# Folding the last layer's conditioning columns on VectorE ahead of one matmul with ones

## The chip, the cores and the metric

The kernel runs on 1 core of a Trainium2 chip, in one launch. The metric is the device time of one execution in microseconds; the kernel before was timed in three runs.

## The reference

A backbone of two layers over 256 latent tokens and 256 context tokens of 1024 channels, all in float32. Each layer takes a conditioning vector `c`, turns it into six vectors of 1024 (shift, scale and gate for each of two sub-layers), and uses them around a token mixer and a mixture of experts:

```
silu_c = silu(c)
for layer in range(2):
    mx = split(silu_c @ ada_w[layer] + ada_b[layer], 6)      # ada_w[layer] is 1024 x 6144
    hx = rms_norm(x, g0) * (1 + mx[1]) + mx[0]
    z = hx @ w_in[layer]                                     # 1024 x 1952: queries, keys, values of four head groups
    o = mix(z) @ w_out[layer]
    x = x + mx[2] * rms_norm(o, g1)
    h = rms_norm(x, g2) * (1 + mx[4]) + mx[3]
    x = x + mx[5] * rms_norm(moe(h), g3)                     # 16 experts, 2 of one group per token
```

The context tokens go the same way with a conditioning vector of their own, but in the last layer they only give keys and values. So of the last layer's six vectors the context stream uses only the first two.

## The kernel before

Each layer runs as a chain of stages: input projection (`project`), second projections of the latent head group (`latent_projections`), attention (`mix`), output projection (`project_out`), routing, experts, and `combine`, which adds the experts' rows and prepares the next layer's tokens. Layer 1 is the last one.

The conditioning is a product of a 2 x 1024 matrix with a 1024 x 6144 one. The weight matrix `ada_w[L]` is cut into 12 items of 2 MB, `("ada", L, i)`. Three rounds `r` of four items give 2048 columns each: r=0 shift and scale of the mixer, r=1 gate of the mixer and shift of the experts, r=2 scale and gate of the experts. In one item the channel index of partition p is 8p + k, with two values of k. `ada_item` (L464) does one item on TensorE: for both k and four column groups g, a matmul with the 32 columns of `silu_c` as the stationary operand and 512 weight columns as the moving one, accumulated in one PSUM bank (B_ADA). Each float32 matmul shows as two instructions in the trace, so an item has 16. After four items VectorE copies the bank to SBUF (`ada_rows`, L1290), TensorE turns it in four transposes (`ada_turn`, L483), and VectorE adds the bias and makes the gains (`ada_columns`, L1298 to L1311).

For layer 1, round 0 is done in layer 0's attention. Items 4 to 11 are done between the layers and in layer 1's input projection: item 4 ahead of `turn_combined(L, 0)`, items 5 and 6 after the tiles cq0 and cq1, item 7 at the end of the first weight chunk, item 8 after the second, items 9 and 10 after the third, item 11 after the fourth.

The order between the layers is this. `combine` has two halves: the latent tokens (s=0) and the context tokens (s=1). For each, VectorE adds the experts' rows and normalises (L1642 to L1669), with row statistics from ScalarE (L1204 to L1208, L965 to L969). TensorE then turns the rows (`turn_combined`, L884), and ScalarE applies scale and shift on the way out of PSUM (`modulate_combined`, L994). Input projections of layer 1 follow in four weight chunks: cq0, cq1, ckv, kr | bk, bv, bq0, bq1 | dq0, dk0, dq1, dk1 | dv0, dv1, u0, u1. Of cq, bq, dq and u only the 256 latent tokens are computed, of the others all 512. The engines run their programs in order and wait on semaphores for named events: "staged" (a weight item has landed), "used" (its buffer may be overwritten), "filled" and "read" (a PSUM bank).

SyncE issues all weight loads in one queue, in the order of `items`. The six staging buffers are thirds of `W[0]` (0 to 2) and `W[1]` (3 to 5), 16 KB a partition each. A load waits for "used" of the item that had the buffer last. `R1` is a region of 4096 columns that holds the experts' rows in `combine`, and later, in attention, the probabilities. Layer 1's queries, keys and values are written into `W[0]`, that is over the staging buffers 0 to 2.

On VectorE, layer 1 starts with `ada_rows(1, 1)` and `ada_columns(1, 1)`, then `latents` (the gains of cq and ckv, L1336 and L1339), then `ada_rows(1, 2)`, then the rotary embeddings (`rope`, L1321 to L1330, with the copies at L1346).

Of the kernel before, what the change touches and what calls it, by code (L numbers as in the profile page):

```python
# [24 lines left out]
D = 1024  # L25
# [137 lines left out]
def hybrid_block(nc, A, out, known=None):  # L163
    ctx = ExitStack()
    with ctx:
# [70 lines left out]


        h_scaled = [part(R1, i * D, D) for i in range(2)]
        amp2_row, gate1_row = part(R1, 2 * D, D), part(R1, 3 * D, D)
# [138 lines left out]
        for L in range(DEPTH):  # L378
# [4 lines left out]
            for i in range(HEADS):  # L383
# [9 lines left out]
        stage1 = [(("in", 1, 0), 3), (("in", 1, 1), 4), (("in", 1, 2), 5), (("ada", 1, 4), 1), (("ada", 1, 5), 2),  # L393
                  (("ada", 1, 6), 1), (("ada", 1, 7), 0), (("in", 1, 3), 3), (("ada", 1, 8), 0), (("ada", 1, 9), 4),
                  (("ada", 1, 10), 0), (("ada", 1, 11), 5), (("out", 1, 0), 3), (("out", 1, 1), 4)]
        items += [it for it, _ in stage1]
# [40 lines left out]
        def _(pe):  # L437
# [25 lines left out]
            def ada_item(S, it):  # L463
# [12 lines left out]
                mm.then_inc(*mark(S, ("used", item_no[it])))  # L476

            def ada_turn(S, L, r):

                pe.wait_ge(*at("ada_sb", L, r))  # L480
                t = take("adaT", L, r)
                for q in range(4):
                    mm = nc.tensor.transpose(t[:, q * P:(q + 1) * P], ada_sb[:, q * P:(q + 1) * P], ident)  # L483
                mm.then_inc(*mark(S, ("filled", "adaT", L, r)))

            def project(L):
# [25 lines left out]
                for c, names in enumerate((("cq0", "cq1", "ckv", "kr"), ("bk", "bv", "bq0", "bq1"),  # L512
# [4 lines left out]
                    if c == 0 and L:  # L517

                        for name in ("cq0", "cq1"):
                            tile(name, w, take(name, L), 0, SEQ).then_inc(*mark(S, ("filled", name, L)))  # L520
                        for i in (5, 6):
                            ada_item(S + "_ada", ("ada", 1, i))
                        turn_combined("pe_comb1", L, 1)
                        t = {name: take(name, L) for name in ("ckv", "kr")}
                        for lo in (0, SEQ):
                            for name in ("ckv", "kr"):
                                mm = tile(name, w, t[name], lo, lo + SEQ)
                                if lo:
                                    used = [("used", item_no[it])] if name == "kr" else []
                                    mm.then_inc(*mark(S, ("filled", name, L), *used))  # L530
                        ada_item(S + "_ada", ("ada", 1, 7))
                        continue
                    for name in names:
# [13 lines left out]
                        if used and L == 0 and c:  # L547
                            ada_item(S + "_ada", ("ada", 0, 3 + c))
                        if used and L:
                            for i in {1: (8,), 2: (9, 10), 3: (11,)}[c]:  # L550
                                ada_item(S + "_ada", ("ada", 1, i))
                            if c == 1:
                                ada_turn(S + "_turn", 1, 1)
                        if name == "bk":
# [354 lines left out]
            for L in range(DEPTH):  # L909
                if L:  # L910
                    ada_item("pe_comb", ("ada", 1, 4))
                    pe.wait_ge(*at("banks_out", L - 1))
                    turn_combined("pe_comb", L, 0)
# [26 lines left out]
        def _(act):  # L940
# [61 lines left out]
            def project(L):  # L1002
# [10 lines left out]
                for g in range(4):  # L1013
                    keys = [("read", "kr", L), ("tile", L, "kr")] if g == 3 else []
                    a(kr[64:96, g * P:(g + 1) * P], src[MLA_ROPE * g:MLA_ROPE * (g + 1), 0:P], ACT.Copy).then_inc(*mark(S, *keys))
                copy(S, bks[L], ("bk", L), keys=[("tile", L, "bk")])
                finish_rstd(S, ("cq", L), 1, (0, nq), 256, ("ckvn", L - 1) if L else None)
                square(S, ("ckv", L), 0, ckv, NTOK, 0)
                copy(S, bvs[L][:, :, :].rearrange("p t c -> p (t c)"), ("bv", L), keys=[("v", L, "swa")])
                for j in range(2):  # L1020
                    src = read(act, f"bq{j}", L)
                    for b in range(2 if nq > SEQ else 0):
                        a(bqz[L][64 * b:64 * b + 64, 2 * b + j, SEQ:nq], src[64 * b:64 * b + 64, SEQ:nq], ACT.Copy, scale=SWA_SCALE)
                    a(bqs[L][:, j, :], src[:, 0:SEQ], ACT.Copy, scale=SWA_SCALE)\
                        .then_inc(*mark(S, ("read", f"bq{j}", L), ("tile", L, f"bq{j}")))
                finish_rstd(S, ("ckv", L), 0, (0, NTOK), 128, ("cqn", L))
                for j in range(2):
                    copy(S, dqs[L][:, j, 0, 0:nq], (f"dq{j}", L), nq, scale=DIFF_SCALE, keys=[("tile", L, f"dq{j}")])
# [14 lines left out]
            def latent_projections(L):  # L1043
                S, nq = f"act_lat{L}", q_tokens(L)
                for h in range(HEADS):
                    copy(S, qas[L][0:MLA_QK, h, 0:nq], ("qa", L, h), nq, hi=MLA_QK, scale=MLA_SCALE, keys=[("tile", L, f"qa{h}")])
# [234 lines left out]
        def _(v):  # L1281
# [3 lines left out]
            def ada_rows(S, L, r):  # L1285

                v.wait_ge(*at("used", item_no[("ada", L, 4 * r + 3)]))
                if (L, r) != (0, 0):
                    v.wait_ge(*at("filled", "adaT", *((L, r - 1) if r else (L - 1, 2))))
                nc.vector.tensor_copy(ada_sb[:, :], psum[:, B_ADA, :]).then_inc(*mark(S, ("ada_sb", L, r)))  # L1290

            def ada_columns(S, L, r):
# [39 lines left out]
            def latents(L):  # L1332
# [6 lines left out]
                stt(ckv, ckv, vecT[:, 68 + L:69 + L], rstd[:, :], ALU.mult, ALU.mult).then_inc(*mark(S, ("ckvn", L)))  # L1339
                if L:  # L1340
                    ada_rows(S, 1, 2)
                rope(S, L, "kr")
# [377 lines left out]
            for L in range(DEPTH):  # L1720
                if L:
                    ada_rows("v_seam", 1, 1)
                    ada_columns("v_seam", 1, 1)
                latents(L)
# [10 lines left out]
        def _(g_):  # L1735
            gt = nc.gpsimd.tensor_tensor

            def zero_queries(L):

                g_.wait_ge(*at("filled", "ckv", L))  # L1740
                nc.gpsimd.memset(bqz[L][64:P, 0:2, :], 0.0)
                nc.gpsimd.memset(bqz[L][0:64, 2:4, :], 0.0).then_inc(*mark(f"g_rope{L}", ("q_zero", L)))
# [161 lines left out]
        def _(sp):  # L1904
# [26 lines left out]
            for L in range(DEPTH):  # L1931
# [16 lines left out]
                for n in range(lo, hi):  # L1948
                    if items[n] == ("ada", 1, 7):
                        for tt in range(4):  # L1950
# [62 lines left out]
```

## Time and profile before

| What | Value |
|---|---|
| Runs | 1197.90, 1199.62, 1202.74 us (median 1199.62) |
| Profiled execution | 1200.96 us, of which the trace's span is 1199.1 |
| TensorE matmul busy | 950.8 us, 79% |
| VectorE busy | 316.3 us, 26% |
| ScalarE busy | 266.5 us, 22% |
| GpSimd busy | 171.0 us, 14% |
| DMA, mean over the span | 269 GB/s |
| Mean granted TensorE clock | 0.903 |

A granted clock of 1.00 is 2.4 GHz, one of 0.50 is 1.2 GHz. "Busy" says how long an engine had an instruction under way; what bounds a stage is read from which wait ends last in it. The change lies between 680 and 800 us of the span; the experts of layer 0 lie before it, attention and the experts of layer 1 behind it.

### The profile page before, as it was taken

How to read it: one execution, taken by the hardware profiler on the slowest of the kernel's cores; microseconds unless marked ns; L12 is line 12 of the kernel's file. 1: busy time of each engine (PE TensorE's matmuls, PEld its weight loads, DVE VectorE, ACT ScalarE, POOL GpSimd, SP SyncE). 2: the span in 40 equal slices, each digit the busy share in tenths (PEclk: the TensorE clock that was granted, in tenths of full speed). 3: DMA queues.
4: the chain of work that ended last, by engine and by line, in shares of the span. 5: the costliest groups of instructions: out<-in, count | busy, mean ns of one | idle time of the engine just before them, and what ended most of it. 6: DMA issues, size and time to landing. Idle time of an engine off the chain costs nothing. (4 is left out here: it accounts for less than half of the span.)

```text
span 1199.1 us, 23394 instructions
## 1 busy us (share of the span) xinstructions
PE 950.8 (79%) x8976; PEld 601.0 (50%) x8977; DVE 316.3 (26%) x893; ACT 266.5 (22%) x712; POOL 171.0 (14%) x256
## 2 busy tenths in 40 slices
PE   4899998999997699989974289998996585655561
PEld 2454646766554466656752166657754353422240
DVE  1100064457434211111110420046635110000003
ACT  4121033546332111101100241024632100000001
POOL 0010025000021222211210220013001211100011
PEclk9999997999997799999997599998997788877796
DMA  9982333570175799999999945230129999999983
GB/s 376 333 254 101 140 141 141 211 247 1 34 283 208 274 372 410 410 411 410 411 411 404 357 160 234 107 140 1 38 89 371 374 410 409 410 410 410 409 326 136
DMA packets 97333, 323.04 MB, mean 269 GB/s; under 512 B 11946, under 2 KB 22964, under 8 KB 90996
## 3 DMA queue, kind: packets, MB, share of 16 engines
q1 hardware_dynamic: 70528, 279.19, 59.0%
q0 software_dynamic: 9600, 31.81, 7.8%
q10 hardware_dynamic: 17140, 11.13, 3.0%
q8 instruction: 46, 0.75, 0.2%
q14 instruction: 19, 0.16, 0.0%
HBM read 309.58 MB, written 18.81 MB: 274 GB/s over the span
## 5 line engine op out<-in xcount | busy, mean ns | idle before, releaser
L825 PE MATMUL psum<-weights,lat 128*32 128x256 f32 x2688 | 181.3, 426 | 96.7 <-DMA weights<-in_exp_w_gu_dram 59.5
L825 PEld LDWEIGHTS psum<-weights,lat 128*32 128x32 f32 x2688 | 108.8, 121 | 163.9 <-issue 131.5
L508 PE MATMUL psum<-hT,weights 128*128 128x512 f32 (+1 forms) x336 | 120.7, 518 | 5.6 <-ACT lat L1000 3.2
L1607 DVE STREAM_TRANSPOSE lat<-lat 128x256 f32<-128x256 f32 x66 | 29.4, 446 | 355.1 <-PE psum L825 342.6
L1169 ACT ACTIVATE lat<-psum 128x128 f32<-128x128 f32 x64 | 17.7, 277 | 357.6 <-PE psum L825 355.4
L508 PEld LDWEIGHTS psum<-hT,weights 128*128 128x128 f32 x336 | 64.0, 192 | 59.3 <-issue 49.1
L838 PE MATMUL psum<-weights,lat 128*32 128x256 f32 x1344 | 83.7, 387 | 4.7 <-issue 4.0
L659 PE MATMUL psum<-weights,R 128*128 128x64 f32 x480 | 68.8, 286 | 11.3 <-ACT R L1084 7.1
L1851 POOL DMA_INDIRECT lat<-h_rows,slot_col x68 | 66.5, 978 | 53.9 <-POOL slot_col L1848 53.0
L1380 DVE TENSOR_REDUCE st<-psum 128x1 f32<-128x512 f32 (+1 forms) x96 | 56.7, 599 | 61.9 <-PE psum L628 28.3
L659 PEld LDWEIGHTS psum<-weights,R 128*128 128x128 f32 x480 | 64.2, 205 | 16.1 <-ACT R L1084 10.9
L474 PE MATMUL psum<-weights,silu_c 128*32 128x512 f32 x384 | 49.2, 634 | 29.1 <-DMA weights<-in_ada_w_dram 29.1
L838 PEld LDWEIGHTS psum<-weights,lat 128*32 128x32 f32 x1344 | 53.5, 112 | 26.8 <-issue 6.5
L1071 ACT ACTIVATE R<-psum,st 128x512 f32<-128x512 f32 (+1 forms) x78 | 48.0, 616 | 84.8 <-DVE st L1380 53.3
L737 PE MATMUL psum<-weights,hT 128*128 128x512 f32 x144 | 65.3, 608 | 0.2 <-ACT hT L1108 0.2
L1848 POOL COPY slot_col<-slots 128x1 int32 (+1 forms) x68 | 12.4, 183 | 366.3 <-DVE lat L1607 348.8
L825 PE MATMUL psum<-hT,lat 128*32 128x256 f32 x672 | 46.3, 418 | 22.8 <-DMA hT<-in_exp_w_gu_dram 10.7
L825 PE MATMUL psum<-R,lat 128*32 128x256 f32 x672 | 43.7, 399 | 8.9 <-DMA R<-in_exp_w_gu_dram 8.9
L1175 ACT ACTIVATE lat<-psum 128x256 f32<-128x256 f32 x63 | 24.1, 383 | 102.6 <-PE psum L838 101.0
L825 PEld LDWEIGHTS psum<-hT,lat 128*32 128x32 f32 x672 | 26.6, 118 | 39.0 <-issue 31.4
L1000 ACT ACTIVATE weights<-psum 128x512 f32<-128x512 f32 (+4 forms) x36 | 20.1, 559 | 112.9 <-PE psum L508 51.0
L737 PEld LDWEIGHTS psum<-weights,hT 128*128 128x128 f32 x144 | 27.5, 195 | 32.4 <-issue 32.1
(260 smaller groups left out, 1161.0 us busy)
## 6 DMA issues: line engine op xcount, KB each, us to landing
weights<-in_exp_w_gu_dram SPq DMA_DIRECT2D x44, 2048.0 KB, 23.9
weights<-in_ada_w_dram SPq DMA_DIRECT2D x24, 2048.0 KB, 8.7
weights<-in_exp_w_down_dram SPq DMA_DIRECT2D x22, 2048.0 KB
hT<-in_exp_w_gu_dram SPq DMA_DIRECT2D x10, 2048.0 KB
R<-in_exp_w_gu_dram SPq DMA_DIRECT2D x10, 2048.0 KB, 25.7
spare_w<-in_exp_w_down_dram SPq DMA_DIRECT2D x10, 2048.0 KB, 24.3
weights<-in_w_in_dram SPq DMA_DIRECT2D x6, 2048.0 KB, 16.5
weights<-in_w_out_dram SPq DMA_DIRECT2D x4, 2048.0 KB, 9.1
```

Of the source, the lines that this page charges most:

```text
L474: mm = nc.tensor.matmul(psum[32 * g:32 * g + 32, B_ADA, :], silu_c[:, k, :], w[:, k2, g, :], start=(k == 0), stop=(k == 7), skip_group_che ...
L508: mm = nc.tensor.matmul(t[:, lo:hi], w[:, k, col:col + P], hT[:, k, lo:hi], start=(k == 0), stop=(k == KD - 1))
L659: mm = nc.tensor.matmul(t[:, 0:64], probT[u % 2][:, i, :], v, start=(i == 0), stop=(i == n - 1))
L737: nc.tensor.matmul(t, mixT[:, k, tt * P:(tt + 1) * P], w[:, k, :], start=(k == 0), stop=False)
L825: mm = nc.tensor.matmul(gu_ps[BLK * j:BLK * j + BLK, 0:256], xgT[:, k, :], w[:, k % 4, j, :, :, :], start=(k == 0), stop=(k == KD - 1), sk ...
L838: mm = nc.tensor.matmul(y_ps[BLK * j:BLK * j + BLK, 0:256], actT[:, b, :], w_dn[place][:, b, j * 256:(j + 1) * 256], start=(b == 0), stop= ...
L1000: a(dst, src, ACT.Copy, scale=scale).then_inc(*mark(S, ("read", *job), *keys))
L1071: a((prob[u % (AHEAD + 1)] if v == 0 else prob2)[:, 0:nk], read(act, "s", L, u, v)[:, 0:nk], ACT.Exp, bias=s_[:, v:v + 1], accum_out=s_[:, ...
L1175: a(y_sb[par], psum[:, 3, 0:256], ACT.Copy).then_inc(y_copied, 1)
L1380: ins = red(s_[:, j:j + 1], read(v, "s", L, u, j)[:, 0:nk], AX.X, ALU.max, negate=True)
L1607: nc.vector.transpose(xgT[:, :, :].rearrange("p k s -> p (k s)"), xg[par]).then_inc(x_ready, 1)
L1851: g_.indirect_dma_start(xg[par], None, h_parts, bass.IndirectOffsetOnAxis(ap=slot_col[:, par:par + 1], axis=0))\
```

## The change

For items 4 to 11 of layer 1, TensorE's matmuls are taken out. VectorE instead multiplies each weight block of 128 partitions x 2048 columns by the one column of `silu_c` that belongs to it and adds it to an accumulator of 128 x 2048 in `R1` (`ada_fold`: one tensor_scalar and seven scalar_tensor_tensor a round). Then four matmuls with 32 columns of ones sum the accumulator over the partitions into bank B_ADA (`ada_sum`). Only the latent stream's vectors come out, which is all that the last layer uses of these rounds. The copy, the turn and the columns stay, at other places. The staging buffers of items 6, 7, 11 and of the second output weights change, "used" of an ada item is now told by VectorE, and ScalarE and GpSimd get waits where they write over a staging buffer.

```diff
+        ada_acc = part(R1, 0, 2 * D)
...
-        stage1 = [(("in", 1, 0), 3), (("in", 1, 1), 4), (("in", 1, 2), 5), (("ada", 1, 4), 1), (("ada", 1, 5), 2),
-                  (("ada", 1, 6), 1), (("ada", 1, 7), 0), (("in", 1, 3), 3), (("ada", 1, 8), 0), (("ada", 1, 9), 4),
-                  (("ada", 1, 10), 0), (("ada", 1, 11), 5), (("out", 1, 0), 3), (("out", 1, 1), 4)]
+        stage1 = [(("in", 1, 0), 3), (("in", 1, 1), 4), (("in", 1, 2), 5), (("ada", 1, 4), 1), (("ada", 1, 5), 2),
+                  (("ada", 1, 6), 0), (("ada", 1, 7), 2), (("in", 1, 3), 3), (("ada", 1, 8), 0), (("ada", 1, 9), 4),
+                  (("ada", 1, 10), 0), (("ada", 1, 11), 4), (("out", 1, 0), 3), (("out", 1, 1), 5)]
...
+            def ada_sum(S, L, r):
+                pe.wait_ge(*at("folded", L, r))
+                reuse(B_ADA, ("ada_sb", L, r))
+                for g in range(4):
+                    mm = nc.tensor.matmul(psum[32 * g:32 * g + 32, B_ADA, :], ones[:, 0:32], ada_acc[:, g * 512:(g + 1) * 512],
+                                          start=True, stop=True, skip_group_check=True)
+                mm.then_inc(*mark(S, ("ada_sum", L, r)))
...
-                        for i in (5, 6):
-                            ada_item(S + "_ada", ("ada", 1, i))
...
-                        ada_item(S + "_ada", ("ada", 1, 7))
...
-                        if used and L:
-                            for i in {1: (8,), 2: (9, 10), 3: (11,)}[c]:
-                                ada_item(S + "_ada", ("ada", 1, i))
-                            if c == 1:
-                                ada_turn(S + "_turn", 1, 1)
+                        if L and name == "bq0":
+                            ada_sum(S + "_ada", 1, 1)
+                        if L and name == "dk1":
+                            ada_turn(S + "_turn", 1, 1)
+                        if L and name == "dv0":
+                            ada_sum(S + "_ada", 1, 2)
...
-                    ada_item("pe_comb", ("ada", 1, 4))
...
+                if L:
+                    act.wait_ge(*at("used", item_no[("ada", 1, 4)]))
                 copy(S, bks[L], ("bk", L), keys=[("tile", L, "bk")])
...
+                if L:
+                    act.wait_ge(*at("used", item_no[("ada", 1, 7)]))
                 for j in range(2):
                     copy(S, dqs[L][:, j, 0, 0:nq], (f"dq{j}", L), nq, scale=DIFF_SCALE, keys=[("tile", L, f"dq{j}")])
...
+                if L:
+                    act.wait_ge(*at("used", item_no[("ada", 1, 10)]))
                 for h in range(HEADS):
                     copy(S, qas[L][0:MLA_QK, h, 0:nq], ("qa", L, h), nq, hi=MLA_QK, scale=MLA_SCALE, keys=[("tile", L, f"qa{h}")])
...
+            def ada_fold(S, L, r):
+                for k in range(KD):
+                    it = ("ada", L, 4 * r + k // 2)
+                    w, c = staged(it)[:, k % 2, :, :].rearrange("p g n -> p (g n)"), silu_c[:, k, 0:1]
+                    used = [("used", item_no[it])] if k % 2 else []
+                    if k % 2 == 0:
+                        v.wait_ge(*at("staged", item_no[it]))
+                    if k == 0:
+                        ts(ada_acc, w, c, None, ALU.mult).then_inc(*mark(S, ("fold", L, r, k)))
+                    else:
+                        v.wait_ge(*at("fold", L, r, k - 1))
+                        stt(ada_acc, w, c, ada_acc, ALU.mult, ALU.add)\
+                            .then_inc(*mark(S, ("fold", L, r, k), *used, *([("folded", L, r)] if k == KD - 1 else [])))
...
                 if L:
+                    ada_rows(S, 1, 1)
+                    ada_fold(S, 1, 2)
+                    ada_columns(S, 1, 1)
                     ada_rows(S, 1, 2)
                 rope(S, L, "kr")
...
                 if L:
-                    ada_rows("v_seam", 1, 1)
-                    ada_columns("v_seam", 1, 1)
+                    v.wait_ge(*at("filled", "yT", 1, 0, KD // 2 - 1))
+                    ada_fold("v_seam", 1, 1)
                 latents(L)
...
                 g_.wait_ge(*at("filled", "ckv", L))
+                if L:
+                    g_.wait_ge(*at("used", item_no[("ada", 1, 4)]))
...
-                    if items[n] == ("ada", 1, 7):
+                    if items[n] == ("ada", 1, 6):
                         for tt in range(4):
                             sp.wait_ge(*at("x", 0, 2, tt))
                     load(n)
```

## Rows read from the trace of the kernel before

**Rows 1.** Page, busy time, share of the span and instructions of each engine.

```profile
PE 950.8 (79%) x8976; PEld 601.0 (50%) x8977; DVE 316.3 (26%) x893; ACT 266.5 (22%) x712; POOL 171.0 (14%) x256
```

**Rows 2.** Chain of waits, 600 to 960 us: start, us, what, instructions.

```profile
705.66 3.69 PE psum L508 x16
...
716.75 1.72 PE psum L474 x14
718.46 7.06 PE psum L508 x16
...
740.59 1.85 PE psum L474 x16
...
743.89 20.64 PE psum L508 x64
764.53 3.57 PE psum L474 x32
768.10 14.01 PE psum L541 x64
...
789.02 1.90 PE psum L474 x16
790.94 0.55 DVE spare_w L1290
```

**Rows 3.** Timeline, seam between the layers: start us, us, engine, line, idle before.

```profile
680.22 0.75 DVE L1669 TENSOR_SCALAR R<-x_tok,rs 128x1024 f32<-128x1024 f32 x1 [1.12 <-ACT rs L969]
...
682.94 3.64 PE L474 MATMUL psum<-weights,silu_c 128*32 128x512 f32 x16 [28.35 <-DMA weights<-in_ada_w_dram]
...
686.51 2.15 PE L884 MATMUL psum<-cst,R 128*128 128x128 f32 x16
...
687.46 3.75 ACT L994 ACTIVATE hT<-psum,mod,amp 128x256 f32<-128x256 f32 x8 [7.26 <-PE psum L884]
...
688.50 7.07 PE L508 MATMUL psum<-hT,weights 128*128 128x256 f32 x32
...
691.06 1.09 ACT L1204 ACTIVATE spare_w<-spare_w 128x1024 f32<-128x1024 f32 x1
...
695.50 3.64 PE L474 MATMUL psum<-weights,silu_c 128*32 128x512 f32 x32
...
699.68 0.75 DVE L1669 TENSOR_SCALAR spare_w<-x_tok,rs 128x1024 f32<-128x1024 f32 x1 [1.11 <-ACT rs L969]
```

**Rows 4.** TensorE by stretches: length, busy, instructions, granted clock, DMA share, GB/s.

```profile
625.00:626.00 1.00, 0.00 (x0) 0.75 1.06 414
823.00:824.00 1.00, 0.47 (x2) 0.74 0.00 0
682.90:686.50 3.60, 3.56 (x16) 0.50 0.94 396
699.20:705.60 6.40, 1.94 (x16) 1.00 0.94 370
1000.00:1050.00 50.00, 29.13 (x468) 0.86 1.03 410
```

**Rows 5.** VectorE groups by form: busy us, mean ns; idle before.

```profile
L1645 DVE SCALAR_TENSOR_TENSOR R<-R,rs 128x1024 f32<-128x1024 f32 x4 | 5.1, 1284 | 3.0 <-DMA R<-y_rows,spos 3.0
...
L1339 DVE SCALAR_TENSOR_TENSOR lat<-lat,vecT,spare_w 128x512 f32<-128x512 f32 x2 | 1.5, 752 | 24.0 <-ACT spare_w L959 24.0
```

**Rows 6.** Timeline, 803 to 806 us: VectorE additions without and with GpSimd beside them.

```profile
804.50 0.42 DVE L1330 TENSOR_TENSOR weights<-R 96x256 f32<-96x256 f32 x1
...
805.09 0.63 POOL L1755 TENSOR_TENSOR R<-weights,cst 96x256 f32<-96x256 f32 x1 [5.90 <-DVE weights L1330]
805.29 0.72 DVE L1330 TENSOR_TENSOR weights<-R 96x256 f32<-96x256 f32 x1
```

**Rows 7.** Staged loads: all of L1912, and those of the conditioning, 620 to 1000 us.

```profile
DMA to landing us min/median/max: 7.2/10.3/33.0
...
weights<-in_ada_w_dram SPq DMA_DIRECT2D x8, 2048.0 KB, 9.5
```

More of the change, by code:

```diff
@@ L1285, in ada_rows @@
             def ada_rows(S, L, r):
-                v.wait_ge(*at("used", item_no[("ada", L, 4 * r + 3)]))
+                if L and r:
+                    v.wait_ge(*at("ada_sum", L, r))
+                else:
+                    v.wait_ge(*at("used", item_no[("ada", L, 4 * r + 3)]))
                 if (L, r) != (0, 0):
@@ L1290, in ada_rows @@
                 nc.vector.tensor_copy(ada_sb[:, :], psum[:, B_ADA, :]).then_inc(*mark(S, ("ada_sb", L, r)))
+            def ada_fold(S, L, r):
[7 more added lines that the diff above has]
+                        ts(ada_acc, w, c, None, ALU.mult).then_inc(*mark(S, ("fold", L, r, k)))
+                    else:
+                        v.wait_ge(*at("fold", L, r, k - 1))
+                        stt(ada_acc, w, c, ada_acc, ALU.mult, ALU.add)\
+                            .then_inc(*mark(S, ("fold", L, r, k), *used, *([("folded", L, r)] if k == KD - 1 else [])))
             def ada_columns(S, L, r):
```

## The prediction

> **What bounds the kernel now.** The page comes first: TensorE is busy for 79% of the span [rows 1], a mean over stages that differ. The chain of waits from 600 to 960 us shows the stage that is touched: from 705.66 to 790.94 it is TensorE alone, input-projection matmuls with the conditioning's (L474) between them, with no wait for another engine [rows 2]. What goes from TensorE there, goes from the path. The timeline of the seam shows the stretch before it [rows 3]. TensorE's first work of the layer is item 4, which waits for its load until 682.94, while the rows for the first turn are ready after VectorE's 680.22 + 0.75 = 680.97. The turn (L884) starts at 686.51. ScalarE modulates behind it until 691.21, and only then takes the statistics of the context rows (691.06), because its program runs in order; these lead to the last scaled rows at 700.43, and to the projection at 705.66. Attention follows from 790.94. Layer 1's experts move weights at 410 GB/s with the DMA engines full (share 1.03) [rows 4]; their first loads wait for the end of attention, so the whole DMA-bound stretch moves with it and gives nothing back.
>
> **Item 4 leaves the seam.** The turn can start at about 681.05 in place of 686.51: 5.46 us earlier. But item 4's 3.64 us ran at a granted clock of 0.50 [rows 3, 4], that is 1.2 GHz, and the turn behind it at 2.4 GHz. Now the turn itself meets the low clock. Its 2.15 us become about 4.3; ScalarE follows one bank behind, so its 3.75 us of modulation end some 0.7 us later against the turn's start. 5.46 - 0.7 = 4.76 us are left for the chain through ScalarE and VectorE to 705.66.
>
> **Items 5 and 6** (695.50, 3.64 us) lie where TensorE would otherwise wait for the scaled rows until 700.43 [rows 3]. Removed, they give nothing.
>
> But TensorE is now busy less. Its projection of cq ends near 693 to 694; then it waits to about 695.7, turns for 1.94 us, and waits some 3.2 us more for ScalarE. In the trace the clock fell at 625 and at 823, in or just after idle gaps of 2 to 3 us, but held through 699.20 to 705.60, which had 1.94 us of work in 6.40 [rows 4]. The new stretch is 1 to 2 us longer with the same work in it. I take it that the clock falls once. Where it fell, it came back after 3 to 7 us; 3.2 us of projection at half rate lose 1.6 us, and the chance that the second turn is caught as well adds 0.2. The bounds are 0 and 3.5 (a fall of 7 us). I take 1.8, since the projection that follows is dense. 4.76 - 1.8 = **2.96 us**.
>
> **Items 7 to 11 leave the projection.** They are on the path at 1.71 (716.75 to 718.46), 1.86, 3.57 and 1.90 us [rows 2]: 9.04. The two sums bring back four matmuls of 512 columns each, half an item, so half of 1.85: 0.9 each, 1.8 together. The turn of round 1 (0.6 us) only moves. 9.04 - 1.8 = **7.2 us**.
>
> **VectorE's copy leaves the path.** Before, rope waited behind the copy of 0.55 us that followed item 11 at 790.94 [rows 2]. Now the second sum is done two tiles earlier, and VectorE waits for the rotation of kr itself. That gives about **0.45 us**; bounds 0 and 0.6.
>
> **The folds and their cover.** Two forms bound the price: scalar_tensor_tensor takes 1284 ns for 1024 columns and 752 for 512 [rows 5], so 1.04 ns a column plus 0.22, and 2.35 us for 2048. The first step, with one tensor operand, takes 0.75 us for 1024 [rows 3], so between 1.3 and 1.5. A fold is 1.4 + 7 x 2.38 = 18 us. VectorE is idle for most of the stage, so this costs nothing if each fold is ready when its sum is due.
>
> The first starts at about 697.5 - 1.8 = 695.7, behind the scaled rows. Item 6 now waits for the last x rows (near 693) and lands by 702. Item 7 waits on SyncE for the buffer of item 5, that is for the fourth step (704.4); queued behind it are the last input chunk, which waits for its own buffer until about 712 anyway, and item 8. Item 7 lands 7.2 to 9.5 us after its issue [rows 7], near 712 to 714, so the fold ends at 717 to 719. Its sum is due after bq0: 11.1 us of first chunk, then 22.1 - 1.9 - 3.5 us, near 732. Cover: 12 us. Queued behind it on VectorE are the gains of cq, which need statistics that are not ready before about 720.
>
> The second starts after ckv's gain and the copy of round 1, near 740.6, and ends at 758.4 if nothing lacks. Its items form a chain. Item 9 waits for the second chunk's buffer (736.8) and lands at 744.0 to 746.3, where step 3 is due at 744.3. Item 10 waits for step 2 (744.3) and lands at 751.5 to 753.8. Item 11 takes item 9's buffer, so it waits for step 4 (749 to 751) and lands at 756 to 760.5. The fold ends at 761 to 765.5. Its sum is due after dv0: the third chunk's 20.64, 0.6 of turn and 7.0 of dv0 [rows 2] after 737.7, near 765.9. Cover: 0.4 to 4.9 us. So it costs nothing, narrowly.
>
> The added waits of ScalarE and GpSimd are for items 4 and 7 (done by 700 and 719, asked at about 720 and 739) and item 10 (done near 757, asked near 780): nothing. The larger accumulator is written over rows of R1 that are used up, and gone before attention's probabilities.
>
> **A rule against the change.** A VectorE addition of 256 columns takes 0.42 us alone and 0.72 with a GpSimd operation beside it [rows 6]. The Trainium skill's "GPSIMD Engine Reference", section 1, says that GpSimd shares its SBUF interfaces with VectorE, with contention for VectorE instructions that have two SBUF inputs; seven of the eight steps are such. By that rule the folds could stretch wherever GpSimd works; this trace agrees for short additions.
> By rows 6 alone a step beside GpSimd work would take 0.72 / 0.42 = 1.7 times as long. In the first fold GpSimd has about 2.3 us of work (two fills and two cosines), which adds 1 to 2 us inside a cover of 12. In the second it has none, because its next cosine waits for kr's rope.
>
> **Sum.** 2.96 + 7.2 + 0.45 = 10.6 us. The profiled execution took 1200.96, so its like would take 1190.4; the three runs' median is 1.34 lower, which puts the median at 1189.0.
>
> **Rivals.**
> - The clock does not fall in the seam: 12.4 us gained, 1187.2. For it speaks 699.20 to 705.60, against it the two other gaps [rows 4].
> - The second fold is late: loads land slower than 9.5 us, which the maximum of 33.0 shows possible [rows 7], though the DMA engines are nearly free here; or steps take 1.7 times as long [rows 6], which makes the fold 31 us and its end near 772. TensorE then waits 3 to 7 us at the second sum, and everything behind waits too: 1192 to 1196, say 1194.5.
> - The seam gives nothing: another wait takes item 4's place in front of the turn. I see none (bank release is long past), but then 7.6 us remain: 1192.
> - Slower: the steps on 2048 columns run far slower than the slope of two shorter forms says. The second fold ends at 740.6 + 8 steps; the gain is eaten when it ends 10.6 us after 765.9, that is at 4.5 us a step, and 6 us more are lost at 5.2. Price at 6 us a step: 740.6 + 48 = 788.6, 22.7 late, 12 us slower: 1212. Nothing in [rows 5] points to it.
>
> **How the numbers follow.** Forecast 0.49; no fall 0.29; late fold 0.12; seam without gain 0.06; slower 0.04. A measurement of this kernel tells about 0.5% from no change, so faster means under 1193.6: the first two, the fourth, and part of the third, less some doubt for the sizes: 0.85. Within 0.5%: 0.11. Slower: 0.04. The range takes in the second case with 2.5 us of spread below and the late fold's middle above: 1184.5 to 1195.
>
> **What would show it.** In the changed trace: the first L884 near 681 at a clock of 0.50; the projection of ckv starting near 702.7 (700.9 without a fall); steps of 2.35 us; TensorE without a gap at both sums; rotation of kr near 780; then attention's end and the first expert load some 10.6 us earlier. The prediction is wrong if TensorE is idle before the second sum, if steps are longer, or if the clock stays low past 706.

## The result and the profile after

The changed kernel took 1183.36 us (median of four runs, 1181.96 to 1188.72); the kernel before beside it took 1198.76 (four runs, 1195.94 to 1202.74). The ratio is 0.9875, with a 95% interval of 0.9839 to 0.9911. Nine further runs of the changed kernel, against 25 of the kernel before, gave a ratio of 0.9917 (0.9884 to 0.9951). The forecast was 1189.0 in a range from 1184.5 to 1195: the direction was right, and the median of the first four runs fell 1.1 us below the range. Where the missing time came from is the question of this document.

The page of the changed kernel, busy time by engine, answers to [rows 1]: TensorE has 15.8 us less, VectorE 35 us more.

```profile
PE 935.0 (79%) x8864; PEld 596.0 (50%) x8865; DVE 351.3 (30%) x909; ACT 267.1 (23%) x712; POOL 172.1 (15%) x256
```

Its chain of waits from 720 us on answers to [rows 2] (start, us, what, instructions; L518, L548 and L510 are the projection's matmuls, L484 is `ada_sum`, L493 the turn, L573 the rotation).

```profile
725.15 0.99 PE psum L484 x8
726.15 3.60 PE psum L510 x32
729.75 1.05 PE psum L461 x2
730.81 20.64 PE psum L518 x64
751.45 0.44 PE psum L493 x4
751.88 6.91 PE psum L548 x32
758.79 1.00 PE psum L484 x8
759.79 7.10 PE psum L548 x32
766.89 6.91 PE psum L518 x32
773.80 0.56 PE psum L573 x2
```

No item is left on TensorE, each sum takes 1.0 us, and TensorE goes from tile to sum to tile without a wait. The rotation of kr starts at 773.8 where it was 790.8. The timeline of the seam answers to [rows 3]:

```profile
672.81 0.76 DVE L1703 TENSOR_SCALAR R<-x_tok,rs 128x1024 f32<-128x1024 f32 x1 [1.12 <-ACT rs L976]
...
673.83 3.31 PE L892 MATMUL psum<-cst,R 128*128 128x128 f32 x16 [28.67 <-DVE R L1703]
...
675.02 3.76 ACT L1001 ACTIVATE hT<-psum,mod,amp 128x256 f32<-128x256 f32 x8 [2.24 <-PE psum L892]
...
687.93 1.59 DVE L1317 TENSOR_SCALAR R<-weights,silu_c 128x2048 f32<-128x2048 f32 x1
688.11 3.65 PE L892 MATMUL psum<-cst,spare_w 128*128 128x128 f32 x16 [4.07 <-DVE spare_w L1703]
...
689.55 12.03 DVE L1320 SCALAR_TENSOR_TENSOR R<-weights,silu_c,R 128x2048 f32<-128x2048 f32 x5
...
693.71 5.38 PE L518 MATMUL psum<-hT,weights 128*128 128x256 f32 x16 [1.95 <-ACT lat L1007]
```

The first turn now starts 0.26 us after its rows (673.57) and not 5.54 us after. The first ckv tiles take 5.38 us where they took 3.69. TensorE by stretches shows why, as in [rows 4] (length, busy times of the engines, granted clock, DMA share, GB/s):

```profile
676.00:686.00 10.00, 8.04 (x39) 6.86 (x38) 6.96 (x7) 7.99 (x20) 0.23 (x1) 0.97 0.12 51
686.00:697.00 11.00, 6.94 (x24) 5.97 (x25) 9.60 (x7) 6.08 (x16) 6.13 (x8) 0.54 0.78 265
698.00:706.00 8.00, 8.00 (x82) 6.70 (x82) 5.50 (x3) 0.60 (x1) 1.04 (x2) 1.00 0.62 251
```

Behind the first turn the clock fell once, for some 10 us, and came back in the ckv tiles.

To see where the time went, both spans are cut at the same events of the timelines: SyncE's first expert load of layer 0, the scaled rows of the latent stream, the first turn (L884, L892), the last scaled rows, the first ckv tile, the rotation of kr, and the first expert load of layer 1.

| Stretch, us | before | after | difference |
|---|---|---|---|
| start to first expert load of layer 0 | 325.48 | 318.11 | -7.37 |
| to the scaled rows of the latent stream | 355.49 | 355.46 | -0.03 |
| to the first turn | 5.54 | 0.26 | -5.28 |
| to the last scaled rows | 13.92 | 14.18 | +0.26 |
| to the first ckv tile | 5.23 | 5.70 | +0.47 |
| to the rotation of kr | 85.15 | 80.02 | -5.13 |
| to the first expert load of layer 1 | 99.80 | 99.67 | -0.13 |
| to the end | 308.49 | 307.80 | -0.69 |
| span | 1199.1 | 1181.2 | -17.9 |

The five stretches from the scaled rows to layer 1's first expert load hold the change, and in this pair of profiles they are 9.8 us shorter. The largest difference, 7.37 us, lies in the first quarter of the kernel, where the two programs do the same work.

### The profile page after: what moved, and what is told of

It is laid out like the page before. It is cut to its first block and busy times, and to the rows that moved or that the text cites. A ratio compares the mean times of both kernels' runs of the same rounds, so it can differ in the third digit from the quotient of the medians.

```text
span 1181.2 us, 23197 instructions
## 1 busy us (share of the span) xinstructions
PE 935.0 (79%) x8864; PEld 596.0 (50%) x8865; DVE 351.3 (30%) x909; ACT 267.1 (23%) x712; POOL 172.1 (15%) x256
## 5 line engine op out<-in xcount | busy, mean ns | idle before, releaser
L518 PE MATMUL psum<-hT,weights 128*128 128x512 f32 (+1 forms) x336 | 122.4, 524 | 3.5 <-ACT lat L1007 1.9
L518 PEld LDWEIGHTS psum<-hT,weights 128*128 128x128 f32 x336 | 65.2, 196 | 57.2 <-issue 48.3
L667 PE MATMUL psum<-weights,R 128*128 128x64 f32 x480 | 65.6, 277 | 11.4 <-ACT R L1097 7.1
L667 PEld LDWEIGHTS psum<-weights,R 128*128 128x128 f32 x480 | 60.9, 196 | 16.2 <-ACT R L1097 10.9
L833 PE MATMUL psum<-hT,lat 128*32 128x256 f32 x672 | 46.3, 416 | 22.5 <-DMA hT<-in_exp_w_gu_dram 10.6
L1655 DVE STREAM_TRANSPOSE lat<-lat 128x128 f32<-128x128 f32 x64 | 20.0, 312 | 81.6 <-PE psum L846 80.2
```

What stands on the lines that cost most here:

```text
L518: mm = nc.tensor.matmul(t[:, lo:hi], w[:, k, col:col + P], hT[:, k, lo:hi], start=(k == 0), stop=(k == KD - 1))
L667: mm = nc.tensor.matmul(t[:, 0:64], probT[u % 2][:, i, :], v, start=(i == 0), stop=(i == n - 1))
L833: mm = nc.tensor.matmul(gu_ps[BLK * j:BLK * j + BLK, 0:256], xgT[:, k, :], w[:, k % 4, j, :, :, :], start=(k == 0), stop=(k == KD - 1), sk ...
```

## The experiments

### Is the first quarter part of the change?

Theory A: the change is worth what its own stretches show, about 10 us, and the rest is where the TensorE clock falls in layer 0, which differs from run to run. Theory B: the change moves layer 0 too and is worth 15 us. Both kernels were run again, unchanged.

> The kernel before, unchanged, timed against itself. Theory A (the change is worth about 10.5 us, and what the medians show beyond that is where the TensorE clock happens to fall in layer 0, which both kernels share): runs spread over some 1194 to 1203 us, and the first expert load of layer 0 (325.5 us before, 318.1 us in the changed kernel's trace) lies anywhere between 317 and 326. Theory B (the change also moves layer 0 for good): that load stays within 1 us of 325.5 and the runs within 1197 to 1202.

> The changed kernel, unchanged, timed against the kernel before. Theory A: ratio 0.990 to 0.992 (9.5 to 12 us less), with layer 0's first expert load anywhere between 317 and 326 us of the trace. Theory B: ratio 0.987 or less (15 us), with that load again near 318.

The kernel before, against itself: ratio 1.0 (0.9973 to 1.0026). Its twelve runs form two groups: four from 1191.0 to 1192.9 and eight from 1198.3 to 1200.3. Not every set is parted so sharply: beside the fills below, the same kernel also had runs at 1194.4, 1194.6 and 1195.6. The changed kernel: 0.9917 (0.9884 to 0.9951), which at 1198 us is 9.9 us; two runs at 1181.1 and 1181.3 and seven from 1188.3 to 1192.1. Group against group the change is worth 9 to 11 us. In its second profile the changed kernel had its first expert load of layer 0 at 324.40 us, not at 318.11: it does not keep the early one. The kernel before was again late, at 324.29. The range expected for before (1194 to 1203) was too narrow below.

TensorE by stretches, in the first profile of the changed kernel (length, busy, granted clock, DMA share, GB/s):

```profile
184.00:188.00 4.00, 0.23 (x2) 1.00 0.49 209
188.00:192.00 4.00, 4.00 (x15) 0.57 0.01 4
192.00:202.00 10.00, 10.00 (x82) 1.00 0.42 149
```

And in its second profile, the same kernel:

```profile
184.00:188.00 4.00, 0.47 (x3) 0.96 0.43 180
188.00:202.00 14.00, 14.00 (x56) 0.52 0.01 1
202.00:204.00 2.00, 2.00 (x18) 1.00 0.75 176
```

TensorE waits 3.9 us for VectorE in both, and the clock falls within 1 us of the end of that wait in both. In one it comes back within 4 us, in the other it stays at 1.2 GHz for 14 us though TensorE is busy throughout. Of the first ten profiles five had the long one, with the load at 322.9 to 325.5. In the other five, with the load at 316.5 to 318.1, the clock was low for 3 to 4 us in four and for 7 us in one (the seam alone, below). Both kinds are spread over kernels with and without the change.

The long stretch is most of the 7.37 us, but not all. When TensorE comes out of that wait, the kernel before is 0.87 us behind. Over the next attention matmuls, up to the end of the long stretch, it loses 4.9 us more. The last 1.6 us come later, where its clock fell twice before the expert load (0.76 in 285 to 290 us, 0.81 in 305 to 310) and that of the changed kernel once (0.66 in 300 to 305).

### Filling the gap in layer 0

```diff
+                    if L == 0 and i == 6:
+                        for _ in range(4):
+                            nc.tensor.matmul(psum[0:30, B_ADA, :], silu_c[:, 0, 2:32], C("inv_count"), start=False, stop=False, skip_group_check=True)
                     if i > AHEAD:
                         values(i - AHEAD - 1)
```

The columns 2 to 31 of `silu_c` are zero, so this adds zeros. It was put into both kernels.

> The kernel before with TensorE fed in one gap of layer 0: its wait of 3.9 us for VectorE at about 185 us of the trace gets four matmuls of 512 columns with a stationary block of zeros, added to the conditioning bank. In five of the ten profiles so far the clock that falls at that gap stays low for 14 us, in the others for 3 to 4, with the first expert load at 323 to 325.5 or at 316.5 to 318. Theory A (this draw is what splits the runs of every kernel here into two groups 7 us apart): with the gap filled the clock holds at 1.00 there, the first expert load comes at 318 or earlier, the runs form one group, near 1191 to 1193 where the kernel before has most of them at 1198 to 1200. If the groups come from elsewhere, two groups remain.

> The changed kernel with the same fill in layer 0. Theory A: one group near 1181 to 1182, and against the kernel before with the same fill 10 us less, which is the change's worth without the draw of layer 0 (10.6 predicted). Theory B (the change is worth 15): 15 us less than the kernel before with the fill.

The kernel before with the fill, TensorE by stretches:

```profile
184.00:188.00 4.00, 3.63 (x16) 1.00 0.09 31
188.00:192.00 4.00, 3.42 (x27) 1.00 0.00 0
192.00:202.00 10.00, 10.00 (x84) 1.00 0.58 211
```

The clock holds, there and up to the first expert load, which comes at 313.8 us (313.9 in the changed kernel). Before with the fill: 1191.96 us (twelve runs, ten of them 1188.9 to 1193.9, two at 1196.3 and 1199.0). Its ratio to the unfilled kernel beside it is 0.9969 (0.9945 to 0.9993), a gain of 3.7 us. Changed kernel with the fill: 1180.49 (six runs, 1179.5 to 1185.2), ratio 0.9877 (0.9844 to 0.991) to the unfilled kernel before. Between the two filled kernels the difference of the medians is 11.5 us, of the means 11.0, with a standard error of 1.3 from the spread of the runs (an estimate). So with this draw filled, the change is worth what its own stretches say, and 15 us is unlikely. The fill moves most runs of the kernel before into the lower group, so layer 0's clock accounts for most of the split. It does not remove it: a spread of some 5 us and two runs above it stay, and in the last experiment below the filled kernel still had its load at 317.2, with two later falls of the clock.

The profiles show a second such place, which I had not looked for. In attention of layer 1, too, TensorE has one wait of 2.2 us for ScalarE. In the first profile of the changed kernel (one row of the timeline, one of TensorE by stretches):

```profile
806.27 1.92 PE L667 MATMUL psum<-weights,R 128*128 128x64 f32 x8 [2.22 <-ACT R L1097]
806.20:813.00 6.80, 6.73 (x27) 0.51 0.00 0
```

And at the same place in the kernel of the next experiment:

```profile
814.44 1.10 PE L660 MATMUL psum<-weights,R 128*128 128x64 f32 x8 [2.21 <-ACT R L1084]
814.40:821.20 6.80, 6.76 (x49) 1.00 0.00 0
```

After the same wait the clock fell in one and held in the other. From the rotation of kr to the first expert load of layer 1 the thirteen profiles took 99.5 to 99.9 us (seven), 98.0 (two) or 96.4 to 96.7 (four). This is a draw of up to 3 us inside the stretches that I had counted as the change's own. Both kernels, three profiles each (unchanged, unchanged again, with the fill):

| us | scaled rows to rotation | rotation to expert load | together |
|---|---|---|---|
| before | 109.84, 110.37, 110.05 | 99.80, 99.67, 99.70 | 209.64, 210.04, 209.75 |
| after | 100.16, 99.70, 100.89 | 99.67, 98.02, 97.98 | 199.83, 197.72, 198.87 |

Up to the rotation the means differ by 9.8 us. Together they differ by 11.0, and 1.2 of that is how the clock fell in layer 1's attention. Whether the change makes a fall there less likely, three profiles each do not tell.

### The seam alone

The kernel before, with all items on TensorE, the changed kernel's staging buffers and SyncE's wait at item 6, and this order:

```diff
-                    ada_item("pe_comb", ("ada", 1, 4))
...
-                        for i in (5, 6):
+                        for i in (4, 5):
                             ada_item(S + "_ada", ("ada", 1, i))
...
-                        ada_item(S + "_ada", ("ada", 1, 7))
+                        for i in (6, 7):
+                            ada_item(S + "_ada", ("ada", 1, i))
```

> The kernel before with only the seam changed: all items stay matmuls on TensorE, with the changed kernel's staging buffers; items 4 and 5 come after the cq tiles, 6 and 7 after the first chunk. The first turn starts 0.3 us after its rows where it took 5.5 to 6.3, and items 4 and 5 keep TensorE busy where it would idle. Expected: 5.3 us gained in front of the turn, 0.3 lost behind it (low clock in the turn), item 6 on the path for 1.8: 3.2 us faster than before, 87.0 us from the ckv tiles to the rotation of kr, ckv tiles at full clock (3.7 us for 16). If the fold itself is needed for the seam's gain, no gain.

Ratio 0.9958 (0.9917 to 0.9999). The first turn starts 0.26 us after its rows, so the gain in front of the turn does not need the fold; it needs item 4 out of the way. The last scaled rows follow in 14.17 us. But from the ckv tiles to the rotation it took 89.7 us, not 87.0, and TensorE's timeline shows why:

```profile
683.25 3.64 PE L474 MATMUL psum<-weights,silu_c 128*32 128x512 f32 x32
686.82 1.97 PE L885 MATMUL psum<-cst,spare_w 128*128 128x128 f32 x16
691.98 6.55 PE L508 MATMUL psum<-hT,weights 128*128 128x256 f32 x16 [3.19 <-ACT lat L1000]
```

The ckv tiles ran at the low clock (6.55 us in place of 3.69), in spite of items 4 and 5 in front. The clock fell in the 3.19 us before them, a gap that it had survived in [rows 4]. My expectation that the items would hold it was wrong. There was a second loss. The cq tiles in front took 8.10 us, the clock being low in part of them, so items 4 and 5 ended late and the second turn started 0.87 us after its rows (685.95). From the scaled rows to the rotation this kernel took 110.18 us, against 109.84 in the kernel before: all of the 5.28 us were lost again behind the turn. That the whole was faster still is in line with the two draws: its profile had one of the shorter falls in layer 0 and none in layer 1's attention (96.58 us). So moving the items alone does not keep the gain of the seam; why the clock did not survive the gap here is open.

### Half of the fold

Round 1 folded, round 2 back on TensorE: `ada_fold(S, 1, 2)` and its sum are gone, and

```diff
+                        if L and name == "dk0":
+                            ada_item(S + "_ada", ("ada", 1, 8))
+                        if used and L and c > 1:
+                            for i in {2: (9, 10), 3: (11,)}[c]:
+                                ada_item(S + "_ada", ("ada", 1, i))
```

> The changed kernel with round 2 (items 8 to 11) back on TensorE: item 8 after dk0, 9 and 10 after the third chunk, 11 after the fourth; round 1 stays folded. By the sum, four items (7.33 us) come back, one sum of 1.0 goes, and VectorE's copy of 0.45 stands on the path again: 6.8 us slower than the changed kernel, so some 3.7 us faster than before. If the gain of the folds lay elsewhere than in TensorE's time on the path, it keeps more than half of it (over 6 us faster than before).

Ratio 0.9953 (0.9924 to 0.9982), or 5.6 us faster than before, between the 3.7 expected and the 6 of the alternative; by the time alone this settles nothing. The profile does. From the scaled rows to layer 1's first expert load it takes 205.90 us, 3.74 less than the first profile of the kernel before, with the clock falling in layer 1's attention in both. And from the ckv tiles to the rotation 86.38 us against 80.02 in the changed kernel, 6.36 more, where the sum says 7.33 - 1.0 = 6.33. So the second fold is worth the items it removes.

### How much cover the folds have

Steps that multiply by a column of zeros were put at the end of a fold, four or eight:

```diff
+                    for m in range(extra):
+                        v.wait_ge(*at("fold", L, r, k + m))
+                        stt(ada_acc, w, silu_c[:, k, 2:3], ada_acc, ALU.mult, ALU.add)\
+                            .then_inc(*mark(S, ("fold", L, r, k + m + 1), *((*used, *last) if m == extra - 1 else ())))
```

> The changed kernel with four more steps of 2048 columns at the end of the first fold; they multiply by a column of zeros, so they add nothing. In the changed kernel the first fold ends at 708.8 us of the trace and its sum starts at 725.1, so there are 16 us of cover. If the fold is hidden, 4 x 2.38 = 9.5 us more cost nothing: from the ckv tiles to the rotation of kr 80.0 us as before the addition, total within 1 us. If VectorE is on the path there, 9.5 us more.

> The changed kernel with four more such steps at the end of the second fold. It ended at 756.15 us, and its sum started at 758.72 without TensorE waiting: a cover of 2.6 us. By that, 9.5 us more make TensorE wait 6.9 us at the second sum, and from the ckv tiles to the rotation of kr it takes 86.9 us in place of 80.0. If another wait has room there (the fold waits for its loads), less; if the fold delays anything else on VectorE, more than 9.5.

> Eight more steps at the end of the second fold: 19.0 us more, of which 2.6 are covered, so 16.4 us of waiting at the second sum and 96.4 us from the ckv tiles to the rotation. That eats the change's gain of some 10.5 us and makes the whole about 6 us slower than the kernel before (1204 to 1205 against 1198.5). If the fold's time were not what ends the wait, it would stay faster than before.

First fold: 80.01 us from the ckv tiles to the rotation, as without the steps (80.02). They are free. The four runs (1179.95 to 1192.17, median 1185.91) spread too far to test the total within 1 us.

Second fold, four steps: 86.25 us. TensorE's timeline:

```profile
747.88 7.07 PE L548 MATMUL psum<-weights,hT 128*128 128x256 f32 x32
760.49 1.94 PE L484 MATMUL psum<-R,ones 128*32 128x512 f32 x8 [5.54 <-DVE R L1326]
762.36 2.93 PE L548 MATMUL psum<-weights,hT 128*128 128x256 f32 x6
```

TensorE waits 5.54 us for the fold, and then pays once more: the clock has fallen, so the sum takes 1.94 us and not 1.07, and the 32 matmuls of the next tile 8.61 and not 7.17. Here the ckv tiles had run at the full clock (3.69 us), so the base of this profile is 78.3 us rather than 80.0, and the lateness cost 5.54 + 0.87 + 1.44 = 7.9 us. The wait is 5.54 and not the 6.9 expected because the cover was larger here: the eight real steps ended at 750.89, 4.1 us before TensorE was ready for the sum at 754.95, since the last load kept the fold waiting for 0.75 us and not for 1.91. The ratio is 0.9966 (0.9933 to 0.9999), so some 4 us of the change are left. Eight steps: TensorE waits 14.97 us, 97.7 us to the rotation, and the whole takes 1204.63 us, ratio 1.0036 (1.0001 to 1.0072): 4.3 us slower than the kernel before by the ratio, where 6 were expected. The slower rival was a real mechanism with the price about as worked out; only its condition did not hold.

### Holding the clock in the seam

```diff
+            def warm(n, cols):
+                for _ in range(n):
+                    nc.tensor.matmul(psum[:, B_ADA, 0:cols], ones[:, :], C("band")[:, 0:cols], start=True, stop=True, skip_group_check=True)
...
+                        warm(4, 512)
                         turn_combined("pe_comb1", L, 1)
+                        warm(3, 512)
...
                     pe.wait_ge(*at("banks_out", L - 1))
+                    pe.wait_ge(*at("ada_sb", 1, 0))
+                    pe.wait_ge(*at("x", 0, 2, 0))
+                    warm(5, 256)
                     turn_combined("pe_comb", L, 0)
```

> The changed kernel with TensorE fed where it idles in the seam: matmuls of ones on constants, whose sums nobody reads, 5 of 256 columns ahead of the first turn, 4 of 512 after the cq tiles and 3 of 512 after the second turn. If the low clock in the seam is what costs there, both turns and the ckv tiles run at a granted clock of 1.00: first turn 2.1 us where it took 3.31, second 1.9 where it took 3.65, the ckv tiles 3.7 where they took 5.38; the projection starts its second chunk about 2.4 us sooner after the scaled rows, and the whole is 2 to 2.5 us faster than the changed kernel. If the clock is set by something else, the same durations as in the changed kernel and no gain, or a loss of 1 to 2 us where a filler runs past the wait.

```profile
666.54 4.17 PE L491 MATMUL psum<-cst,ones 128*128 128x256 f32 x10 [21.02 <-DVE x_tok L1698]
671.48 1.94 PE L899 MATMUL psum<-cst,R 128*128 128x128 f32 x16 [0.77 <-DVE R L1713]
673.26 7.07 PE L523 MATMUL psum<-hT,weights 128*128 128x256 f32 x32
680.17 3.60 PE L491 MATMUL psum<-cst,ones 128*128 128x512 f32 x8
685.30 1.94 PE L899 MATMUL psum<-cst,spare_w 128*128 128x128 f32 x16 [1.53 <-DVE spare_w L1713]
687.07 2.74 PE L491 MATMUL psum<-cst,ones 128*128 128x512 f32 x6
690.42 3.69 PE L523 MATMUL psum<-hT,weights 128*128 128x256 f32 x16 [0.61 <-ACT lat L1017]
```

In this timeline of TensorE both turns take 1.94 us and the ckv tiles 3.69, and no filler runs past the wait that it fills. Against the first profile of the changed kernel, the turn's start is 0.16 us sooner, the last scaled rows 0.47, the ckv tiles 0.47, the rotation 1.68: 2.8 us in all, where 2.4 were expected. Median 1180.89, ratio to before 0.9869 (0.983 to 0.9907); six runs, three of them 1177.3 to 1177.8 and three 1184.0 to 1187.5, which looks like the draw of layer 0 again. By the two ratios this is 5.8 us faster than the changed kernel, more than the 2 to 2.5 expected. The profile shows where more came from: from the rotation to the expert load it takes 96.67 us in place of 99.67, the clock holding in layer 1's attention. It did so in both profiles with these fillers, but also in two of the eleven without them, so that it is their doing is not shown. Then the fill of layer 0 was added:

> The changed kernel with the fillers of the seam and the fill of layer 0 together. If both are independent: one group near 1177 to 1178, the lower edge of what the seam's fillers alone gave (1177.3 to 1187.5), and 21 us faster than the kernel before.

Median 1176.61 (1173.8 to 1181.2), ratio 0.9838 (0.9804 to 0.9872): about 19 us faster than the kernel before, the best version here. The gain was 20.5 by the medians, 21 expected; the spread of 7 us is wider than the one group that I expected. In its profile the clock held at the filled wait (1.00 from 184 to 204 us), but fell later, to a mean of 0.72 in 278 to 284 and in 299 to 305 us, and the load came at 317.2. So the fill takes out the long fall and not the later ones, which the two other profiles with the fill did not have. Against the changed kernel with the same fill it is 3.9 us faster by the medians.

## Why the prediction was right in its parts and missed its range

**The step that failed** is the last one: "the three runs' median is 1.34 lower, which puts the median at 1189.0", and a range made only from cases inside the changed stretches. It took the level of the kernel before for fixed, and so put what the clock does outside the changed stretches at nothing. The level has two values some 7 us apart, mostly from the clock in layer 0. Of the first four runs of before three were in the upper group (1197.9 to 1202.7) and one between the groups (1195.9); of the first four of the changed kernel three were in the lower (1182.0 to 1183.7). Of the 15.4 us between those medians some 10 to 11 are the change and 4 to 5 the draw, an estimate from the runs with the fill. Which group a run falls into is chance as far as these runs show; with a sample like the nine later runs the median would have been 1189.9, inside the range. A range with both groups would have reached to about 1181. The hint stood in [rows 4]: I used the falls of the clock for the seam alone, and did not ask what the same falls do to the rest of the kernel. And the sentence that the clock "came back after 3 to 7 us" was already untrue of the trace of before, where it was low for 13.7 us from 188.6 on, with TensorE busy.

**Item 4 out of the seam.** Predicted 5.46 us in front of the turn, measured 5.28. Right, and confirmed by the seam alone (0.26 us from rows to turn).

**The low clock in the first turn.** Predicted 0.7 us, measured 0.26. The turn took 3.31 us and not 4.3 (3.65 in the profiles in which the clock was low for all of it). ScalarE's modulation took as long as before (3.76 us, 3.75 before) and only started 0.24 us later behind the turn's start, so it, and not the turn, sets the pace.

**The fall in the seam.** Predicted one fall at 1.8 us. In the first profile 0.47 in front of ckv and 1.7 in its tiles, 2.2 together; without a fall (the fillers) none of it. The low clock lasted 10 us and not 3 to 7, but TensorE was idle for a part of them. It is not in every execution: with four steps more in the second fold the ckv tiles ran at full clock.

**Items 5 and 6.** They were hidden, as said; the wait before the second turn grew to 4.07 us.

**Items 7 to 11 and the sums.** Predicted 7.2 us. From the ckv tiles to the rotation 5.13 went, and the low clock there cost 1.7, so 6.8; the fillers show it directly, 85.15 to 78.34 = 6.8. The sums cost 1.0 each and not 0.9, and the second dv tile takes 7.17 us in place of some 7.04.

**VectorE's copy.** Predicted 0.45 us, measured 0.13 between the rotation and the first expert load. The overlap was wrong: the copy, from 790.94 to 791.63, ran beside the rotation's own matmuls (790.81 to 791.42), for which rope has to wait anyway. Rope started 0.85 us behind the rotation's start before, and 0.65 after: only 0.20 us of the copy was on the path.

**The folds' price and cover.** The steps of the changed kernel, by source line (duration min, median, max in ns):

```profile
L1320 DVE SCALAR_TENSOR_TENSOR R<-weights,silu_c,R x14: 2350/2352/2352, 689.6 to 753.8; 128x2048 f32<-128x2048 f32 x14
its engine sat idle before it (us, times) until:
  DMA weights<-in_ada_w_dram: 7.1, 3
```

2352 ns against 2350 worked out from the two shorter forms. The fold waited three times for a load, 7.1 us in all, at the places named (items 7, 10, 11). The first ended at 708.8, 16 us before its sum (12 predicted). Part of that difference is a slip in the prediction's sum: its "22.1 - 1.9 - 3.5" takes item 8 off a stretch (718.46 to 740.59) in which it does not lie. Without the 1.9 the sum is due near 734, a cover of 14. The second fold ended at 756.15, 2.6 us before its sum (0.4 to 4.9 predicted). That this cover is real and thin, the added steps show: 9.5 us more made TensorE wait 5.5, a cover of 4 us in that execution. The 1 to 2 us by which GpSimd was to stretch the first fold did not come: all fourteen steps of this profile take 2.35 us.

**The sum.** 10.6 predicted; 9.8 in the changed stretches of the first profiles, 9.9 by the ratio of the longer comparison, 11.0 to 11.5 with layer 0's wait filled. That these agree so well is in part luck: the terms missed by up to 0.4 us each, and layer 1's attention adds a draw of its own.

## What to carry to other kernels

Before a range is set around a gain of 1%, look at the runs of the kernel before as a set and at the granted clock over the whole span: a stretch that the change does not touch can have two durations, and three runs do not show both. A matrix-vector product that sits between dense matmuls can go to an idle VectorE, step by step into one accumulator with one short matmul of ones at the end; its worth is the TensorE time it removes, provided that the fold ends before its sum is due. Here the landing of the last load decided that, and not the arithmetic. Where TensorE waits a few microseconds in front of dense work, matmuls that nobody reads can hold the clock for it: here 2.8 us in the seam, and some 4 us for one filled wait of 3.9 us.

## What the hardware showed that was not expected

- The length of a low-clock stretch is not set by the work behind it. After the same 3.9 us wait in layer 0 it was 3 to 4 us, 7 us or 14 us, with TensorE busy at once in all; the long one costs 5 us of a kernel of 1198, and some 7 with what differs around it. After the same 2.2 us wait in layer 1 the clock fell in some executions and held in others.
- Turns alone can lift the clock. In the changed kernel the first turn began at 673.83 at a clock of 0.50, and the clock was 1.00 from some 676.6, while the first matmul behind the turn started at 676.97. In six other profiles the same turn passed at the low clock (3.64 or 3.65 us), and the clock rose only in the cq tiles.
- Beside the fold it was mostly GpSimd that got slower and not VectorE. In the first profile all 14 steps took 2350 to 2352 ns, while GpSimd's cosine of kr took 1.53 us where it took 0.63 in the kernel before. In other executions both paid: with the seam's fillers one step took 2609 ns beside a cosine of 1.42 us, and of the four steps added to the first fold the slowest took 2609 ns, with the cosine of bk beside them at 2.40 us in place of 0.64. From the changed kernel's timeline:

```profile
704.05 4.74 DVE L1320 SCALAR_TENSOR_TENSOR R<-weights,silu_c,R 128x2048 f32<-128x2048 f32 x2 [2.46 <-DMA weights<-in_ada_w_dram]
...
707.75 1.53 POOL L1791 TENSOR_TENSOR R<-lat,cst 32x256 f32<-32x256 f32 x1 [2.01 <-ACT lat L1022]
```

  In [rows 6] it was the other way round, a VectorE addition of 0.42 us taking 0.72. By the Trainium skill's "GPSIMD Engine Reference", section 1, the two contend where VectorE's instruction has two SBUF inputs; which of them pays is not said there. Here it was VectorE in one case, GpSimd in another, and both in some executions.
